# Gathering the tensor engine's small pieces of attention work in a two-layer hybrid trunk

## The chip, the cores and the metric

The kernel runs on one core of a Trainium2 chip. The metric is the device time of one execution in microseconds (us), from its first to its last instruction and what lies around them.

## The reference

Two layers, each a mixer sub-layer and a gated feed-forward, on x of 512 positions by 1024 channels, all in float32:

```python
for l in range(2):
    h = rms_norm(x, pre_mix_g[l])
    z = h @ w_in[l]                       # 1024 -> [u 512 | v 512 | q 512 | k 512 | values 512]
    u, v = gelu(z[u and v]); v = layer_norm(v)
    y_a = u * (W_s @ v + b)               # 4 groups, 128-position blocks, W_s block-lower-triangular
    # differential attention, 4 heads, two score maps a head (64 channels each), rotary on q and k,
    # 128-row blocks i = 0..3, chunk-causal mask of 64:
    p0, p1 = softmax(mask(q0 k0^T)), softmax(mask(q1 k1^T))
    y_b = rms_norm((p0 - lam * p1) @ values) * (1 - lam_init)
    x = x + rms_norm(concat(y_a, y_b) @ w_out[l])
    h = rms_norm(x)
    x = x + rms_norm((silu(h @ w_gate) * (h @ w_up)) @ w_down)
```

## The kernel before, in words

**Products.** A float32 product is made of three passes in fp32r: each operand is split in a high part and a low rest (`xg_hi`, `xg_lo`, `w_hi`, `w_lo`), and `product` (lines 604 to 606) issues high by high, high by low, low by high. These are the kernel's large matmuls, 512 columns wide in the mixer; this text calls them F. ScalarE makes `w_hi` from the raw weights (`high`, line 1078), GpSimd the rest (`low`, line 535), and SyncE's queue brings the weights, a chunk ahead.

**Small pieces.** The rest of TensorE's work in the mixer is small and lies between stretches of F. A score step n = 4 h + i (head h, row block i, 128 (i + 1) keys wide) goes through this chain:

- `scores(n)` on TensorE (line 669, "S" with its number): three fp32r passes for both maps into two PSUM banks.
- `maxima(n)` on VectorE (lines 1604, 1606): masks and takes the row maxima. `exponentials(n)` on ScalarE (line 1237). `combine(n)` on VectorE (lines 1613 to 1620): p0 - lam p1 into `attn`; its semaphore is `a_ready`.
- `turn(n)` on TensorE (line 682, "T"): i + 1 transposes of 128x128 in fp32. `copy_turned(n)` on ScalarE (lines 1246, 1249); its semaphore is `at_copied`. Steps i = 0 and i = 1 are copied together.
- `weigh(m)` on TensorE (line 697, "W"): steps 2m and 2m + 1 times the values, in fp32 (6 instructions for even m, 14 for odd m). `take_heads(m)` on ScalarE (lines 1258, 1259) takes the result out of the bank and sums its squares.

Each group g of the spatial gating has `gate(g)` (line 707, "G", 8 instructions), `add_terms(g)` on VectorE (line 1638, semaphore `gm_added`), and on u `copy_u(g)` and `u_gelus(g)` on ScalarE (lines 1269, 1273), `gated(g)` on GpSimd (line 542), `gated_high(g)` on ScalarE (line 1279) and `gated_low(g)` on GpSimd (line 546, semaphore `ya_ready`). Each head ends in `head_roots` (line 1264), `scale_head` on VectorE (line 1649, semaphore `o_scaled`), `turn_head(h)` on TensorE (line 714, "H"), `head_high` and `head_low` (lines 1283, 1654, semaphore `yb_ready`).

**The F stretches of the mixer**, in the order of the code: the gate's v, q and k tiles (`qk_half(n, lower or upper)`, 12 F each), the values (`va`), u (`u_half(t, ...)`, 12 F each), and the first half of the output product, `out_k(k)` for k = 0..7, 12 F each; `out_k(k)` waits for `ya_ready` k + 1 (k < 4) or for `yb_ready`. A tile of q or k is rotated after its product: `swapped(n)` on ScalarE (line 1219) waits for the tile's last F, `rotate(n)` on VectorE (lines 1585 to 1591), `rotated_high(n)` (line 1226), `rotated_low(n)` (line 1597, semaphore `qk_ready`).

**Order.** Each engine works through a list written out by hand, in order, once a layer; between them stand only semaphores. Nothing is scheduled at run time: a wait at the head of an engine's list holds all behind it. Before, step n's scores lie in banks 2 and 3 (even n) or 4 and 5 (odd n); bank 6 takes the turned tiles, bank 7 the weighed heads, and `scores(n)` waits for `a_ready` n - 1 (counted in the layer), that is for `combine(n - 2)`.

Of the kernel before, what the change touches and what calls it, by code (L numbers as in the profile page):

```python
# [15 lines left out]
P = 128  # L16
# [4 lines left out]
def trunk(nc, x, pre_mix_g, w_in, gmlp_ln_g, gmlp_ln_b, gmlp_ws, gmlp_b, lambda_q1, lambda_k1, lambda_q2,  # L21
# [41 lines left out]
    SC_BANKS = [(2, 3), (4, 5)]  # L63
    T_BANK, O_BANK = 6, 7

    GATE_BANKS = [2, 3, 4, 5]
# [8 lines left out]
    with ctx:  # L75
# [524 lines left out]
        def _(pe):  # L600
# [50 lines left out]
            def scores(l, n):  # L651
# [4 lines left out]
                if n == 0:  # L656
                    pe.wait_ge(vg_gelu, ST * l + 4)
                elif n == 8 or n == 9:

                    pe.wait_ge(gm_added, G * l + 2 * (n - 7))  # L660
                elif n > 1:

                    pe.wait_ge(a_ready, NS * l + n - 1)

                w = max(w, 2 * P)
                for n_pass, (q, k) in enumerate(((q_rot, k_rot), (q_low, k_rot), (q_rot, k_low))):
                    for j in range(2):
                        ps = slice(j * HD, (j + 1) * HD)
                        last = mm(bank[SC_BANKS[n % 2][j]][:, 0:w], q[ps, h, i * P:(i + 1) * P], k[ps, h, 0:w],  # L669
                                  start=(n_pass == 0), stop=(n_pass == 2))  # L670
                last.then_inc(sc_ready, 1)

            def turn(l, n):
                pe.wait_ge(a_ready, NS * l + n + 1)
                if n == 0:
                    pe.wait_ge(qk_ready, 8 * l + 3)
                elif n % ST != 1:
                    pe.wait_ge(at_copied, NS * l + n)

                at = 1 if n % ST == 1 else 0  # L680
                for k in range(n % ST + 1):
                    last = tr(b_tr[T_BANK][:, at + k, :], attn[n % 2][:, k * P:(k + 1) * P], ident[:, :])  # L682
                last.then_inc(at_ready, 1)

            def weigh(l, m):
# [6 lines left out]
                else:  # L692
                    pe.wait_ge(o_taken, 8 * l + m)
                for n in (2 * m, 2 * m + 1):
                    h, i = divmod(n, ST)
                    for k in range(i + 1):
                        last = mm(bank[O_BANK][:, (n % 2) * P:(n % 2 + 1) * P], attn_t(n, k),  # L697
# [3 lines left out]
            def gate(l, g):  # L701
# [3 lines left out]
                pe.wait_ge(a_ready, NS * l + (7 if g < 2 else 8))  # L705
# [176 lines left out]
            for l in range(L):  # L882
# [68 lines left out]
                turn(l, 2)  # L951
                va(C_VA + 1, 1, (0, 1))
                turn(l, 3)
# [17 lines left out]
                turn(l, 6)  # L971
                weigh(l, 1)
                qk_half(l, 4, upper)
                turn(l, 7)
                weigh(l, 2)
                qk_half(l, 5, lower)
                qk_half(l, 5, upper)
                for g in range(G):
                    gate(l, g)
                weigh(l, 3)  # L980
                qk_half(l, 6, lower)
                qk_half(l, 6, upper)
                scores_of_two(8)
# [6 lines left out]
                turn(l, 10)  # L990
                weigh(l, 4)
                u_half(l, 1, lower)
                turn(l, 11)
# [8 lines left out]
                turn(l, 14)  # L1002
                weigh(l, 6)
                u_half(l, 3, upper)
                turn(l, 15)
                out_k(l, 0)
                out_k(l, 1)
                weigh(l, 7)
                out_k(l, 2)
                turn_head(l, 0)  # L1010
                out_k(l, 3)
                turn_head(l, 1)
                turn_head(l, 2)
# [47 lines left out]
        def _(act):  # L1061
# [130 lines left out]
            for l in range(L):  # L1192
# [36 lines left out]
                def exponentials(n):  # L1229
                    w = (n % ST + 1) * P  # L1230
                    act.wait_ge(max_ready, NS * l + n + 1)
                    if n >= 2:
                        act.wait_ge(a_ready, NS * l + n - 1)
                    for j in range(2):
                        o = bank[SC_BANKS[n % 2][j]][:, 0:w]

# [3 lines left out]
                def copy_turned(n):  # L1240
# [4 lines left out]
                    if n % ST == 1:  # L1245
                        fn(attnT[:, 0:3 * P], bank[T_BANK][:, 0:3 * P], ACT.Copy).then_inc(at_copied, 2)
                    else:
                        w = (n % ST + 1) * P
                        fn(attnT[:, AT_AT[n % ST]:AT_AT[n % ST] + w], bank[T_BANK][:, 0:w], ACT.Copy)\
                            .then_inc(at_copied, 1)  # L1250

                def take_heads(m):

                    act.wait_ge(pv_ready, 8 * l + m + 1)
                    for n in (2 * m, 2 * m + 1):
                        h, i = divmod(n, ST)
                        o = bank[O_BANK][:, (n % 2) * P:(n % 2 + 1) * P]
                        fn(o_rows[:, i, h * P:(h + 1) * P], o, ACT.Copy, scale=rinv[:, n, 0:1])
                        last = fn(junk[:, (n % 2) * P:(n % 2 + 1) * P], o, ACT.Square, scale=rinv[:, n, 0:1], accum_out=o_ssq[:, h, i:i + 1])
# [55 lines left out]
                copy_turned(2)  # L1315
                copy_values(0)
                copy_values(1)
# [614 lines left out]
```

## Time and profile before

| | |
|---|---|
| median of 3 runs | 1087.63 us (1087.49 to 1087.68) |
| span of the profiled execution | 1085.3 us |
| instructions | 17599 |
| TensorE matmuls, busy | 1077.2 us, 99% of the span |
| VectorE / ScalarE / GpSimd busy | 601.7 / 585.8 / 573.9 us |
| chain that ended last | TensorE 99% |
| mean granted TensorE clock | 0.999 |

The profiled execution's span is counted from its first to its last instruction; the device time of the runs is 2.3 us above it. A matmul's duration in the rows overlaps with the next one's: what it costs is the distance from its start to the next one's start, and busy time on TensorE hides short pauses for the same reason.

### The profile page before, as it was taken

How to read it: one execution, taken by the hardware profiler on the slowest of the kernel's cores; microseconds unless marked ns; L12 is line 12 of the kernel's file. 1: busy time of each engine (PE TensorE's matmuls, PEld its weight loads, DVE VectorE, ACT ScalarE, POOL GpSimd, SP SyncE). 2: the span in 40 equal slices, each digit the busy share in tenths (PEclk: the TensorE clock that was granted, in tenths of full speed). 3: DMA queues.
4: the chain of work that ended last, by engine and by line, in shares of the span. 5: the costliest groups of instructions: out<-in, count | busy, mean ns of one | idle time of the engine just before them, and what ended most of it. 6: DMA issues, size and time to landing. Idle time of an engine off the chain costs nothing.

```text
span 1085.3 us, 17599 instructions
## 1 busy us (share of the span) xinstructions
PE 1077.2 (99%) x6840; PEld 968.0 (89%) x6840; DVE 601.7 (55%) x1011; ACT 585.8 (54%) x1143; POOL 573.9 (53%) x450
## 2 busy tenths in 40 slices
PE   8999999999999999999999999999999999999997
PEld 7878888999999999888888888889999999988886
DVE  4374544888888884010345646458888888820103
ACT  6767784666555554221457578656565555531212
POOL 3533264567666665544444234645766666655440
PEclk9999999999999999999999999999999999999999
DMA  8423212424433434522243222242443343263212
GB/s 281 137 65 92 78 56 82 155 79 117 117 97 100 117 100 169 178 97 97 86 143 102 78 79 78 68 125 81 118 117 97 98 117 103 93 215 121 96 55 77
DMA packets 144791, 118.33 MB, mean 109 GB/s; under 512 B 3754, under 2 KB 120004, under 8 KB 144708
## 3 DMA queue, kind: packets, MB, share of 16 engines
q1 hardware_dynamic: 144692, 117.20, 34.3%
q8 instruction: 54, 0.88, 0.3%
q14 instruction: 29, 0.24, 0.1%
q10 hardware_dynamic: 16, 0.00, 0.0%
HBM read 110.90 MB, written 6.29 MB: 108 GB/s over the span
## 4 chain that ended last, share of the span: by engine, by line
PE 99%; ACT 0%; DMA 0%; DVE 0%; issue 0%; DVEq 0%; ACTq 0%
PE banks L604 30%; PE banks L606 30%; PE banks L605 30%; PE banks L669 2%; PE banks L697 2%; PE banks L613 1%; PE banks L682 1%; PE banks L873 1%; PE banks L707 1%; DMA x_rows<-in_x_dram 0%; PE banks L714 0%; ACT junk L1086 0%; PE banks L964 0%; PE banks L958 0%; DVE scratch L1502 0%
## 5 line engine op out<-in xcount | busy, mean ns | idle before, releaser
L535 POOL TENSOR_TENSOR w_lo<-raw,w_hi 128x512 fp32r<-128x512 f32 x204 | 259.6, 1296 | 299.1 <-ACT w_hi L1078 299.1
L553 POOL TENSOR_TENSOR w_lo<-raw,w_hi 128x512 fp32r<-128x512 f32 x200 | 260.8, 1315 | 141.4 <-ACT w_hi L1147 137.0
L604 PE MATMUL banks<-xg_hi,w_hi 128*128 128x256 f32 (+1 forms) x896 | 276.3, 308 | 0.0
L606 PE MATMUL banks<-xg_lo,w_hi 128*128 128x256 f32 (+1 forms) x896 | 274.2, 306 | 0.0
L605 PE MATMUL banks<-xg_hi,w_lo 128*128 128x256 f32 (+1 forms) x896 | 274.0, 306 | 0.0
L1078 ACT ACTIVATE w_hi<-raw 128x1024 fp32r<-128x1024 f32 x102 | 107.0, 1060 | 161.4 <-PE banks L606 146.9
L1147 ACT ACTIVATE w_hi<-raw 128x512 fp32r<-128x512 f32 x200 | 125.1, 630 | 114.8 <-DVE raw L1795 61.1
L606 PEld LDWEIGHTS banks<-xg_lo,w_hi 128*128 128x128 f32 x896 | 171.2, 191 | 7.8
L604 PEld LDWEIGHTS banks<-xg_hi,w_hi 128*128 128x128 f32 x896 | 171.2, 191 | 7.7
L605 PEld LDWEIGHTS banks<-xg_hi,w_lo 128*128 128x128 f32 x896 | 171.3, 191 | 6.9
L604 PE MATMUL banks<-w_hi,hid_hi 128*128 128x512 f32 x352 | 137.2, 390 | 0.0
L606 PE MATMUL banks<-w_lo,hid_hi 128*128 128x512 f32 x352 | 137.0, 389 | 0.0
L605 PE MATMUL banks<-w_hi,hid_lo 128*128 128x512 f32 x352 | 137.0, 389 | 0.0
L604 PE MATMUL banks<-s_part,w_hi 128*128 128x256 f32 x480 | 135.8, 283 | 0.0
L605 PE MATMUL banks<-s_part,w_lo 128*128 128x256 f32 x480 | 135.8, 283 | 0.0
L606 PE MATMUL banks<-s_part,w_hi 128*128 128x256 f32 x480 | 135.8, 283 | 0.0
L604 PEld LDWEIGHTS banks<-s_part,w_hi 128*128 128x128 f32 x480 | 92.2, 192 | 0.0
L605 PEld LDWEIGHTS banks<-s_part,w_lo 128*128 128x128 f32 x480 | 92.2, 192 | 0.0
L606 PEld LDWEIGHTS banks<-s_part,w_hi 128*128 128x128 f32 x480 | 92.2, 192 | 0.0
L1801 DVE TENSOR_TENSOR w_lo<-banks,w_hi 128x512 fp32r<-128x512 f32 x80 | 54.9, 686 | 50.8 <-ACT w_hi L1147 50.8
L1524 DVE TENSOR_TENSOR banks<-banks,gpost 128x512 f32<-128x512 f32 x16 | 10.6, 696 | 126.6 <-ACT junk L1112 126.6
L606 PEld LDWEIGHTS banks<-w_lo,hid_hi 128*128 128x128 f32 x352 | 66.1, 188 | 13.9
(182 smaller groups left out, 1878.5 us busy)
## 6 DMA issues: line engine op xcount, KB each, us to landing
raw<-in_w_gate_up_dram SPq DMA_DIRECT2D x88, 512.0 KB, 4.1
raw<-in_w_down_dram SPq DMA_DIRECT2D x44, 512.0 KB, 3.5
raw<-in_w_in_dram SPq DMA_DIRECT2D x40, 512.0 KB, 3.8
raw<-in_w_out_dram SPq DMA_DIRECT2D x16, 512.0 KB, 3.5
x_spill<-x_rows SPq DMA_DIRECT2D x8, 512.0 KB, 4.3
x_rows<-x_spill SPq DMA_DIRECT2D x8, 512.0 KB, 4.7
x_rows<-in_x_dram SPq DMA_DIRECT2D x4, 512.0 KB, 7.4
out_dram<-x_rows SPq DMA_DIRECT2D x8, 256.0 KB, 2.0
```

The lines of the kernel that those rows point to most:

```text
L535: last = tt(lo[:, piece], raw_half(l, c, h)[:, piece], hi[:, piece].bitcast(F32), ALU.subtract)
L553: tt(lo, full, hi.bitcast(F32), ALU.subtract).then_inc(w_ready, 1)
L604: mm(o, stat[0], mov[0], start=first, stop=False)
L605: mm(o, stat[1], mov[0], start=False, stop=False)
L606: return mm(o, stat[0], mov[1], start=False, stop=last)
L613: last = tr(b_tr[turned_bank(group, r, half)][:, k, :], xn[:, r % 2, at:at + P], ident[:, :])
L669: last = mm(bank[SC_BANKS[n % 2][j]][:, 0:w], q[ps, h, i * P:(i + 1) * P], k[ps, h, 0:w], start=(n_pass == 0), stop=(n_pass == 2))
L682: last = tr(b_tr[T_BANK][:, at + k, :], attn[n % 2][:, k * P:(k + 1) * P], ident[:, :])
L697: last = mm(bank[O_BANK][:, (n % 2) * P:(n % 2 + 1) * P], attn_t(n, k), v_att[:, k, h * P:(h + 1) * P], start=(k == 0), stop=(k == i))
L1078: fn(high_low(l, c, h)[0], raw_half(l, c, h), ACT.Copy).then_inc(w_hi_ready, 1)
L1147: fn(factor(l, f, i)[0], full, ACT.Copy).then_inc(w_hi_ready, 1)
L1801: tt(lo, t_place(l, f, i), hi.bitcast(F32), ALU.subtract).then_inc(t_ready, 1)
```

## The change

The arithmetic stays the same. Three kinds of edit:

- **Banks.** Steps i = 0 and i = 1 of a head share banks 2 and 3 (columns 0 to 127 and 256 to 511), i = 2 uses them again, i = 3 has banks 4 and 5. So `maxima`, `exponentials` and `combine` of i = 0 now wait until step i = 1 has come as far too, and `scores` of i = 2 waits for `a_ready` n, that is for `combine(n - 1)`. Turned tiles of i = 3 go to bank 4, the others to bank 6. The weighed heads use all four quarters of bank 7, so that `weigh(1)` and `weigh(2)` can follow each other. `gate(3)` uses bank 5 after `gate(2)` and waits for `add_terms(2)`.
- **TensorE's order.** T2 and T3, T6 and T7, T10 and T11, T14 and T15 stand together; W1, W2 and three gates follow T7; W3, the last gate, S8 and S9 stand together behind the tile qk 6; T10, T11, W4, S12, S13 are one piece; T14, T15 and W6 come after u's last tile; W7 and H0 to H2 come after `out_k(2)`, and H3 after `out_k(4)`.
- **ScalarE's and VectorE's order** is changed to match: `copy_u(3)`, `copy_turned(14)`, `copy_turned(15)`, `take_heads(6)` now stand in this order before `u_gelus(2)`, `swapped(6)` before `take_heads(3)`, and on VectorE `rotate(6)` and `add_terms(3)` before `maxima(8)`.

The diff, with unchanged lines left out:

```diff
--- before.py
+++ after.py
@@ -60,10 +60,11 @@
...
-    SC_BANKS = [(2, 3), (4, 5)]
-    T_BANK, O_BANK = 6, 7
-
-    GATE_BANKS = [2, 3, 4, 5]
+    SC_AT = [(2, 0), (2, 256), (2, 0), (4, 0)]
+    T_BANKS_OF = [6, 6, 6, 4]
+    O_BANK = 7
+
+    GATE_BANKS = [2, 3, 5, 5]
@@ -655,31 +656,41 @@
...
                     pe.wait_ge(vg_gelu, ST * l + 4)
-                elif n == 8 or n == 9:
-
-                    pe.wait_ge(gm_added, G * l + 2 * (n - 7))
-                elif n > 1:
-
+                elif i == 0:
                     pe.wait_ge(a_ready, NS * l + n - 1)
+                elif i == 2:
+                    pe.wait_ge(a_ready, NS * l + n)
+                elif i == 3 and h > 0:
+
+                    pe.wait_ge(a_ready, NS * l + n - 3)
+                    pe.wait_ge(at_copied, NS * l + n - 3)
+                if h == 2 and i == 0:
+                    pe.wait_ge(gm_added, G * l + 2)
+                elif h == 2 and i == 3:
+                    pe.wait_ge(gm_added, G * l + 4)
                 w = max(w, 2 * P)
+                b, at = SC_AT[i]
                 for n_pass, (q, k) in enumerate(((q_rot, k_rot), (q_low, k_rot), (q_rot, k_low))):
...
                         ps = slice(j * HD, (j + 1) * HD)
-                        last = mm(bank[SC_BANKS[n % 2][j]][:, 0:w], q[ps, h, i * P:(i + 1) * P], k[ps, h, 0:w],
+                        last = mm(bank[b + j][:, at:at + w], q[ps, h, i * P:(i + 1) * P], k[ps, h, 0:w],
                                   start=(n_pass == 0), stop=(n_pass == 2))
...
                 pe.wait_ge(a_ready, NS * l + n + 1)
+                i = n % ST
                 if n == 0:
                     pe.wait_ge(qk_ready, 8 * l + 3)
-                elif n % ST != 1:
+                elif i == 0:
+                    pe.wait_ge(at_copied, NS * l + n - 1)
+                elif i == 2:
                     pe.wait_ge(at_copied, NS * l + n)
-                at = 1 if n % ST == 1 else 0
-                for k in range(n % ST + 1):
-                    last = tr(b_tr[T_BANK][:, at + k, :], attn[n % 2][:, k * P:(k + 1) * P], ident[:, :])
+                at = 1 if i == 1 else 0
+                for k in range(i + 1):
+                    last = tr(b_tr[T_BANKS_OF[i]][:, at + k, :], attn[n % 2][:, k * P:(k + 1) * P], ident[:, :])
                 last.then_inc(at_ready, 1)
@@ -689,12 +700,12 @@
...
                     pe.wait_ge(add_ready, l + 1)
-                else:
+                elif m != 2:
                     pe.wait_ge(o_taken, 8 * l + m)
...
                     for k in range(i + 1):
-                        last = mm(bank[O_BANK][:, (n % 2) * P:(n % 2 + 1) * P], attn_t(n, k),
+                        last = mm(b_tr[O_BANK][:, n % ST, :], attn_t(n, k),
                                   v_att[:, k, h * P:(h + 1) * P], start=(k == 0), stop=(k == i))
@@ -702,7 +713,10 @@
...
-                pe.wait_ge(a_ready, NS * l + (7 if g < 2 else 8))
+                if g < 3:
+                    pe.wait_ge(a_ready, NS * l + (7 if g < 2 else 8))
+                else:
+                    pe.wait_ge(gm_added, G * l + 3)
                 for n in range(ST):
@@ -948,9 +962,8 @@
...
                 va(C_VA + 1, 0, (0, 1))
-                turn(l, 2)
                 va(C_VA + 1, 1, (0, 1))
-                turn(l, 3)
+                turn_two(2)
@@ -968,18 +981,18 @@
...
                 qk_half(l, 4, lower)
-                turn(l, 6)
+                qk_half(l, 4, upper)
+                turn_two(6)
                 weigh(l, 1)
-                qk_half(l, 4, upper)
-                turn(l, 7)
                 weigh(l, 2)
+                for g in range(3):
+                    gate(l, g)
                 qk_half(l, 5, lower)
                 qk_half(l, 5, upper)
-                for g in range(G):
-                    gate(l, g)
-                weigh(l, 3)
                 qk_half(l, 6, lower)
                 qk_half(l, 6, upper)
+                weigh(l, 3)
+                gate(l, 3)
                 scores_of_two(8)
@@ -987,10 +1000,9 @@
...
                 u_half(l, 0, upper)
-                turn(l, 10)
+                u_half(l, 1, lower)
+                turn_two(10)
                 weigh(l, 4)
-                u_half(l, 1, lower)
-                turn(l, 11)
                 scores_of_two(12)
@@ -999,18 +1011,15 @@
...
                 u_half(l, 3, lower)
-                turn(l, 14)
+                u_half(l, 3, upper)
+                turn_two(14)
                 weigh(l, 6)
-                u_half(l, 3, upper)
-                turn(l, 15)
-                out_k(l, 0)
-                out_k(l, 1)
+                for k in range(3):
+                    out_k(l, k)
                 weigh(l, 7)
-                out_k(l, 2)
-                turn_head(l, 0)
+                for h in range(H - 1):
+                    turn_head(l, h)
                 out_k(l, 3)
-                turn_head(l, 1)
-                turn_head(l, 2)
                 out_k(l, 4)
@@ -1228,11 +1237,12 @@
...
                     w = (n % ST + 1) * P
-                    act.wait_ge(max_ready, NS * l + n + 1)
+                    act.wait_ge(max_ready, NS * l + n + (2 if n % ST == 0 else 1))
                     if n >= 2:
                         act.wait_ge(a_ready, NS * l + n - 1)
+                    b, at = SC_AT[n % ST]
                     for j in range(2):
-                        o = bank[SC_BANKS[n % 2][j]][:, 0:w]
+                        o = bank[b + j][:, at:at + w]
@@ -1243,20 +1253,20 @@
...
                     if n % ST == 1:
-                        fn(attnT[:, 0:3 * P], bank[T_BANK][:, 0:3 * P], ACT.Copy).then_inc(at_copied, 2)
+                        fn(attnT[:, 0:3 * P], bank[T_BANKS_OF[1]][:, 0:3 * P], ACT.Copy).then_inc(at_copied, 2)
                     else:
                         w = (n % ST + 1) * P
-                        fn(attnT[:, AT_AT[n % ST]:AT_AT[n % ST] + w], bank[T_BANK][:, 0:w], ACT.Copy)\
+                        fn(attnT[:, AT_AT[n % ST]:AT_AT[n % ST] + w], bank[T_BANKS_OF[n % ST]][:, 0:w], ACT.Copy)\
                             .then_inc(at_copied, 1)
...
-                    act.wait_ge(pv_ready, 8 * l + m + 1)
+                    act.wait_ge(pv_ready, 8 * l + m + (2 if m == 1 else 1))
                     for n in (2 * m, 2 * m + 1):
                         h, i = divmod(n, ST)
-                        o = bank[O_BANK][:, (n % 2) * P:(n % 2 + 1) * P]
+                        o = b_tr[O_BANK][:, n % ST, :]
                         fn(o_rows[:, i, h * P:(h + 1) * P], o, ACT.Copy, scale=rinv[:, n, 0:1])
-                        last = fn(junk[:, (n % 2) * P:(n % 2 + 1) * P], o, ACT.Square, scale=rinv[:, n, 0:1], accum_out=o_ssq[:, h, i:i + 1])
+                        last = fn(junk[:, (n % ST) * P:(n % ST + 1) * P], o, ACT.Square, scale=rinv[:, n, 0:1], accum_out=o_ssq[:, h, i:i + 1])
                     last.then_inc(o_taken, 1)
@@ -1312,9 +1322,9 @@
...
                 rotated_high(3)
-                copy_turned(2)
                 copy_values(0)
                 copy_values(1)
+                copy_turned(2)
                 copy_turned(3)
@@ -1330,21 +1340,21 @@
...
                 high(l, 7, 1)
+                swapped(4)
                 copy_turned(6)
+                copy_turned(7)
                 take_heads(1)
-                swapped(4)
-                copy_turned(7)
                 take_heads(2)
...
                 rotated_high(5)
+                swapped(6)
                 take_heads(3)
-                swapped(6)
+                rotated_high(6)
                 exponentials(8)
                 exponentials(9)
-                rotated_high(6)
                 high(l, 9, 0)
@@ -1353,10 +1363,10 @@
...
                 copy_u(0)
+                high(l, 10, 0)
                 copy_turned(10)
+                copy_turned(11)
                 take_heads(4)
-                high(l, 10, 0)
-                copy_turned(11)
                 exponentials(12)
@@ -1371,20 +1381,20 @@
...
                 gated_high(1)
+                copy_u(3)
                 copy_turned(14)
+                copy_turned(15)
                 take_heads(6)
-                copy_u(3)
-                copy_turned(15)
                 u_gelus(2)
...
                 high(l, 11, 1)
+                high(l, 12, 0)
                 take_heads(7)
...
                 head_high(0)
-                high(l, 12, 0)
                 head_high(1)
@@ -1598,18 +1608,20 @@
...
                 def maxima(n):
-                    b, w = SC_BANKS[n % 2][0], (n % ST + 1) * P
-                    dve.wait_ge(sc_ready, NS * l + n + 1)
-
-                    nc.vector.memset(banks[0:CH, b:b + 2, w - CH:w], NEG_INF).then_inc(sc_masked, 1)
+                    b, at = SC_AT[n % ST]
+                    to = at + (n % ST + 1) * P
+                    dve.wait_ge(sc_ready, NS * l + n + (2 if n % ST == 0 else 1))
+
+                    nc.vector.memset(banks[0:CH, b:b + 2, to - CH:to], NEG_INF).then_inc(sc_masked, 1)
                     dve.wait_ge(sc_masked, NS * l + n + 1)
-                    nc.vector.tensor_reduce(nmx[:, n, :], banks[:, b:b + 2, 0:w], AX_X, ALU.max, negate=True)\
+                    nc.vector.tensor_reduce(nmx[:, n, :], banks[:, b:b + 2, at:to], AX_X, ALU.max, negate=True)\
                         .then_inc(max_ready, 1)
...
+                    b, at = SC_AT[n % ST]
                     w = (n % ST + 1) * P
-                    dve.wait_ge(exp_done, 2 * (NS * l + n + 1))
+                    dve.wait_ge(exp_done, 2 * (NS * l + n + (2 if n % ST == 0 else 1)))
                     nc.vector.reciprocal(rinv[:, n, :], psumr[:, n, :]).then_inc(rinv_ready, 1)
@@ -1617,7 +1629,7 @@
...
                         dve.wait_ge(at_ready, NS * l + n - 1)
-                    stt(attn[n % 2][:, 0:w], bank[SC_BANKS[n % 2][1]][:, 0:w], cw[:, n:n + 1], prob[n % 2][:, 0:w],
+                    stt(attn[n % 2][:, 0:w], bank[b + 1][:, at:at + w], cw[:, n:n + 1], prob[n % 2][:, 0:w],
                         ALU.mult, ALU.add).then_inc(a_ready, 1)
@@ -1710,18 +1722,18 @@
...
                 rotated_low(4)
-                rotate(5)
                 add_terms(0)
                 add_terms(1)
+                add_terms(2)
+                rotate(5)
                 rotated_low(5)
-                add_terms(2)
+                rotate(6)
                 add_terms(3)
...
                 maxima(9)
-                rotate(6)
+                rotated_low(6)
                 combine(8)
                 combine(9)
-                rotated_low(6)
                 maxima(10)
```

## Rows read from the trace of the kernel before

**Rows 1.** The page, busy time of TensorE over the whole span.
```profile
PE 1077.2 (99%) x6840; PEld 968.0 (89%) x6840; DVE 601.7 (55%) x1011; ACT 585.8 (54%) x1143; POOL 573.9 (53%) x450
```

**Rows 2.** Waits on TensorE, whole span: us in total, times, longest us.
```profile
PE banks L613 <- DVE scratch L1498: 1.2, 1, 1.2
```

**Rows 3.** Timeline of TensorE, layer 0, u's last tiles and out: start, us.
```profile
145.30 0.49 PE L682 MATMUL banks<-ident,scratch 128*128 128x128 f32 x3
...
146.22 0.47 PE L604 MATMUL banks<-xg_hi,w_hi 128*128 128x512 f32 x1
...
149.07 0.60 PE L682 MATMUL banks<-ident,scratch 128*128 128x128 f32 x4
...
155.00 1.72 PE L697 MATMUL banks<-v_att,attnT 128*128 128x128 f32 x14
156.48 0.48 PE L604 MATMUL banks<-w_hi,ya_hi 128*128 128x512 f32 x1
...
162.53 1.03 PE L714 MATMUL banks<-ident,o_rows 128*128 128x128 f32 x8
```

**Rows 4.** Timeline of TensorE, layer 0: qk 6, S8, qk 7, S10; six F between its first rows.
```profile
110.06 0.39 PE L606 MATMUL banks<-xg_lo,w_hi 128*128 128x512 f32 x1
...
111.42 0.39 PE L606 MATMUL banks<-xg_lo,w_hi 128*128 128x512 f32 x1
111.73 0.38 PE L669 MATMUL banks<-k_rot,q_rot 64*128 64x256 f32 x2
...
112.64 0.50 PE L604 MATMUL banks<-xg_hi,w_hi 128*128 128x512 f32 x1
...
118.31 0.44 PE L669 MATMUL banks<-k_rot,q_rot 64*128 64x384 f32 x2
```

**Rows 5.** Timeline of VectorE, layer 0, gating terms, steps 8 and 9.
```profile
105.64 1.40 DVE L1638 SCALAR_TENSOR_TENSOR v_gate<-banks,par,add_t 128x512 f32<-128x512 f32 x2
...
112.46 0.17 DVE L1604 MEMSET banks<- 64x128 f32 x1 [3.50 <-PE banks L669]
...
113.30 0.69 DVE L1606 TENSOR_REDUCE nmx<-banks 128x2 f32<-128x512 f32 x1
114.26 0.70 DVE L1585 TENSOR_TENSOR banks<-banks,trig 128x512 f32<-128x512 f32 x1 [0.28 <-ACT swap L1219]
...
116.27 0.15 DVE L1613 RECIPROCAL rinv<-psumr 128x2 f32<-128x2 f32 x1
...
117.53 0.48 DVE L1620 SCALAR_TENSOR_TENSOR scratch<-banks,cw,scratch 128x256 f32<-128x256 f32 x1
```

**Rows 6.** Timeline of ScalarE, layer 0, tile qk 6, steps 8 and 9.
```profile
111.84 2.39 ACT L1219 ACTIVATE swap<-banks 32x512 f32<-32x512 f32 x4 [4.17 <-PE banks L606]
114.26 0.37 ACT L1237 ACTIVATE scratch<-banks,nmx 128x128 f32<-128x128 f32 x1
...
115.76 0.21 ACT L1237 ACTIVATION_READ_ACCUMULATOR banks<-banks,nmx 128x1 f32 x1
```

**Rows 7.** Timeline of ScalarE, layer 0, `take_heads(6)` and the table load for gelu.
```profile
146.50 0.37 ACT L1258 ACTIVATE o_rows<-banks,rinv 128x128 f32<-128x128 f32 x1 [0.18 <-PE banks L697]
...
147.61 0.21 ACT L1259 ACTIVATION_READ_ACCUMULATOR junk<-banks,rinv 128x1 f32 x1
...
150.37 1.28 ACT L1273 ACT_TABLE_LOAD   x1
```

**Rows 8.** Timeline of GpSimd, layer 0, `gated` and `gated_low` of groups 2 and 3.
```profile
152.44 2.54 POOL L542 TENSOR_TENSOR uT<-uT,v_gate 128x512 f32<-128x512 f32 x2 [2.54 <-ACT uT L1273]
155.04 2.60 POOL L546 TENSOR_TENSOR ya_lo<-uT,ya_hi 128x512 fp32r<-128x512 f32 x2
```

**Rows 9.** Timeline of VectorE, layer 0, heads 0 to 2 scaled.
```profile
154.73 6.66 DVE L1649 TENSOR_SCALAR o_rows<-o_rows,o_rs 128x128 f32<-128x128 f32 x12
```

**Rows 10.** Waits of TensorE's weight loads, whole span: us in total, times, longest us.
```profile
PEld banks L682 <- issue: 2.9, 8, 0.4
```

**Rows 11.** Window view, 6 to 8 us; after the busy times: granted clock, DMA, GB/s.
```profile
6.00:8.00 2.00, 1.27 (x11) 1.27 (x12) 1.04 (x3) 1.34 (x3) 1.08 (x1) 1.00 1.00 370
```

## The prediction

> **What bounds the kernel now.** I read the page first, then the waits, then the timelines of the mixer, since the change touches nothing else. TensorE is busy 99% of the span [rows 1], and its longest wait in the whole execution is 1.2 us, at the launch [rows 2]; in the mixer it waits for nobody. VectorE, ScalarE and GpSimd are busy little more than half the time, but the hand-written lists let TensorE meet them with small margins, and what counts here are these margins. So the time can move in two ways only: TensorE's own sequence gets shorter, or it starts to wait. Work saved on another engine is worth nothing by itself. Both layers run the same list, so each term counts twice.
>
> **What gathering saves.** An F costs 0.227 us: six lie between 110.06 and 111.42 [rows 4]. Behind a small piece the stretch of F is longer than that: 12 F from 146.22 to 149.07 take 2.85 us where 12 x 0.227 is 2.72 [rows 3]. So a return to F costs 0.13. Part of it is given back: T of three tiles with W6 takes 0.92 (145.30 to 146.22), while four more transposes behind four others add 1.03 - 0.60 = 0.43, that is 0.108 each, by which nine instructions would take 0.97 [rows 3]. The last small instruction before F is thus cheaper by 0.05, or by 0.07 if a weighing instruction costs 0.110, the value that I take below; so one piece fewer saves some 0.06. Counting the lists: before, a layer has 20 separate pieces between stretches of F; after, 13 (T2 joins T3; T6 W1, T7 W2, the gates with W3 and S8 S9 become two; T10 W4 joins T11 S12 S13; T14 W6 joins T15; W7, H0, H1 H2 become one). Seven fewer, in two layers 14: 14 x 0.06 = 0.8 us. Bounds: nothing, and 14 x 0.13 = 1.8 us. The small instructions themselves are all still there.
>
> **First new wait: S10.** `scores(10)` has i = 2. Before, it waited for `combine(8)`, and S11 for `combine(9)`; now S10 waits for `combine(9)`. In front of it, `swapped(6)`, `rotate(6)` and `add_terms(3)` now stand before `maxima(8)` and the exponentials of steps 8 and 9. Before, `maxima(8)` went ahead as soon as S8 was there (112.46) while ScalarE was still swapping tile 6 (111.84 to 114.23) [rows 5, 6]; these two ran side by side, and now they follow one another. I count from E, the end of the F of qk 6 (111.73 in rows 4).
>
> - VectorE and ScalarE: swap starts at E + 0.2 (0.11 in the rows, where the step from F to S holds some 0.1), 2.42 to the next ScalarE instruction (111.84 to 114.26) [rows 6]; rotate 2.01 (114.26 to 116.27); `add_terms(3)` 0.66 to 0.70 (two take 1.40); `maxima` of 8 and 9 is 113.30 + 0.69 - 112.46 = 1.53 [rows 5]; 0.04 to ScalarE; the exponentials of both, which `combine(8)` now awaits together, 115.76 + 0.21 - 114.26 = 1.71 [rows 6]; 0.04 back; both combines 117.53 + 0.48 - 116.27 = 1.74 [rows 5]. With 0.07 until TensorE starts (an estimate) the sum is E + 10.4.
> - TensorE: W3 and G3, 22 instructions at 0.11, 2.4 us (14 of W7 take 1.48 [rows 3]); 0.1 for the step to S; S8 and S9 0.91 (111.73 to 112.64); qk 7 5.67 (112.64 to 118.31) [rows 4]. It is at S10 at E + 9.1.
>
> TensorE waits 1.3 us, and behind S10 everything on it is held: S11, T8, T9, u. By the same count the earlier order had `combine(9)` at 118.01 [rows 5] against S10 at 118.31 [rows 4], so there was no wait. Bounds: 1.0 and 1.7, since no row shows this sequence as a whole. The later chains start from TensorE's own outputs and move with it, so nothing of this is won back: TensorE has no idle time left to give.
>
> **Second new wait: `out_k(2)`.** It needs `gated_low(2)` on GpSimd, which hangs on `u_gelus(2)` on ScalarE. Now `copy_turned(14)` and `take_heads(6)` stand between `copy_u(3)` and the gelu, and `take_heads(6)` waits for W6, which itself now comes only after u's last tile, T14 and T15. I count from U, the end of u's last F (149.07, where T15 began before [rows 3]).
>
> - ScalarE and GpSimd before: table load for gelu at 150.37 = U + 1.30 [rows 7], `gated_low(2)` from 155.04, half of 2.60 for one of the two: ready at 156.34 = U + 7.27 [rows 8]. TensorE came to `out_k(2)` at 156.48 = U + 7.41 [rows 3], 0.14 later.
> - After: T14 T15 W6 take 0.92 + 0.43 = 1.35 [rows 3]; `take_heads(6)` starts 0.28 behind W6's end (146.50 against 146.22) and holds ScalarE 1.2 (146.50 to about 147.7) [rows 3, 7]. The table load starts at U + 2.8 instead of 1.3, 1.5 us later, and `gated` with both `gated_low` and `gated_high` shifts with it: ready at U + 8.8, seen at 8.86.
> - TensorE after: 1.35, then 24 F with one return, 24 x 0.227 + 0.13 = 5.58, make U + 6.93. W7 no longer stands ahead of `out_k(2)` as filler.
>
> TensorE waits 1.9 us. Bounds: 1.6 and 2.3. Queued behind it are W7 and the heads. H2 needs head 2 scaled: before at 154.73 + 6.66 = 161.39 = U + 12.3 [rows 9], now 1.5 later, U + 13.8; TensorE reaches H2 at 8.86 + 2.85 + 1.56 + 0.86 = U + 14.1. Taken as no wait, 0.3 as its upper bound.
>
> **The other edits, costed at nothing.** The shared banks delay the exponentials of steps 0, 4 and 12 by the maxima of the next step, and the combines with them. For step 12 the sum of the same prices is: S12's start + 0.91 + 0.3 to VectorE, 1.53 + 1.71 + 1.74 and the hand-overs give about + 6.1, against S14 at 0.91 + 5.67 = + 6.6 by [rows 4]. If that cover were gone it would cost up to 0.3. S2 and S6 have their combines by the same count, S2 with hardly any spare; up to 0.1. u's second tile loses the piece T10 W4 ahead of it, 0.92 + 0.13, and comes that much closer behind `rotated_low(7)`; up to 0.2. T6, T7, W1, W2 and the gates move later than their inputs, and G3's wait for `add_terms(2)` is met while qk 6 runs. No DMA is moved on SyncE's queue, and GpSimd's list is unchanged.
>
> **Sum.** 2 x (1.3 + 1.9) - 0.8 = +5.6 us. The profiled execution of before has a span of 1085.3 and runs took 2.3 us more; so a span of 1090.9 and a time of 1087.63 + 5.6 = 1093.2 us. Its own range: 2 x 2.6 - 1.8 = +3.4 to 2 x (1.7 + 2.3 + 0.3) = +8.6, that is 1091.0 to 1096.2.
>
> **Rivals.** A measurement of this kernel tells 0.2% (2.2 us) from no change.
>
> - *Only one wait is real* (9%). The two chains are separate. If GpSimd and ScalarE are late as computed but VectorE makes S10 in time: 2 x 1.9 - 0.8, 1090.6. If only S10 waits: 2 x 1.3 - 0.8, 1089.4, within 0.2%. For it: I added single prices. Against it: the spare before was 0.14 and 0.3, and each chain grows by over a microsecond.
> - *Not slower: the pieces cost much more than I take* (5%). The weight loads pause 0.36 us at a transpose piece (2.9 us in 8 cases [rows 10]). If that is what a piece costs, gathering gives 14 x 0.36 = 5.0, and the time is 1087.6 + 6.4 - 5.0 = 1089.0. It decides from 0.30 per piece (inside 0.2%), break-even at 0.46. Against it: the starts of the matmuls, not of the loads, set the time, and these show 0.13 at most.
> - *Faster or the same: the waits don't bind* (4%). If VectorE and ScalarE are released earlier than their lists say, only the saving stays: 1086.8, at best 1085.8.
> - *The clock falls in the pauses* (4%). After a wait of 1.2 us [rows 2] the granted clock stood at 1.00, the level of 2.4 GHz, in the window from 6 to 8 us [rows 11]. The new waits are longer, 1.9. If TensorE fell to 1.2 GHz after each of the four for as long as ten F, each would cost 10 x 0.227 = 2.3 more: 1102.4. The Trainium skill (TensorE: Matmul & The Clock Gate, "HAM oscillation — how this bites in real kernels") says that pauses between bursts of matmuls can put the engine back to the half clock; so far as this trace goes it stays up.
>
> **How the numbers follow.** Forecast 78%, the rivals 9, 5, 4 and 4%. The range of 8 in 10 is 1089.9 to 1096.4: it takes in the forecast's bounds and the case with the second wait alone. Slower by over 0.2%: 78 + 6 (of the first rival) + 4 = 88%. Within 0.2%: 9%. Faster: 3%.
>
> **What would show it.** In the profile after: TensorE with waits in the mixer, in each layer one before S10 (line of the scores, released by VectorE's last combine instruction) of some 1.3 us, and one before the F of `out_k(2)`, released by GpSimd's `gated_low`, of 1.9. 12 F behind a piece still take 2.85, and a layer has 13 pieces. The table load for the second gelu starts 2.8 us after u's last F. Wrong would be: TensorE without idle time in the mixer; a wait at H2, W7 or u's second tile of over half a microsecond; the stretches of F shorter by more than 0.13 for each piece gone; a mean clock visibly below 1.

## The result: 1097.82 us, and the profile after

The changed kernel takes **1097.82 us** (4 runs, 1097.72 to 1097.97), the kernel before 1087.6 us beside it: a ratio of 1.0094 (95% interval 1.0082 to 1.0106). It is slower, as forecast, but by 10.2 us and not by 5.6; the time lies above the range given.

The page of the profiled execution after; its span is 1095.7 us, 10.4 above that of before. It answers to [rows 1]:

```profile
PE 1081.6 (99%) x6840; PEld 971.8 (89%) x6840; DVE 601.9 (55%) x1011; ACT 583.6 (53%) x1143; POOL 574.4 (52%) x450
```

This line tells little: the share of TensorE is the same, and its busy time is 4.4 us longer although it does the same 6840 matmuls. The waits on TensorE (us in total, times, longest), against [rows 2]:

```profile
PE banks L605 <- POOL ya_lo L547: 3.9, 2, 2.0
PE banks L677 <- DVE scratch L1632: 2.6, 2, 1.3
PE banks L857 <- DVE eps L1493: 1.2, 1, 1.2
```

The third is at the launch and is 1.2 us in the kernel before too; the launch wait that [rows 2] shows is 0.5 here. The first two are the two waits forecast, at `out_k(2)` and at S10. Together they are 6.5 us, and gathering takes something off; so some 4 us of the slowdown are in no row of this view. To find them I measured the stretches from the start of one matmul to the start of another, the same ones in both traces. From the first score step to the first F behind H3, before takes 112.91 us in layer 0 and 112.75 in layer 1, after 117.93 and 117.91; every other stretch agrees within 0.1 us. So all of it is in the attention part, 5.0 to 5.2 us a layer. Now TensorE after, layer 0, behind the second wait (start, us, and in brackets the idle time and its releaser), against the rows from 156.48 on in [rows 3]:

```profile
117.78 0.39 PE L607 MATMUL banks<-xg_lo,w_hi 128*128 128x512 f32 x1
119.49 0.45 PE L677 MATMUL banks<-k_rot,q_rot 64*128 64x384 f32 x2 [1.32 <-DVE scratch L1632]
...
155.86 0.39 PE L607 MATMUL banks<-w_lo,ya_hi 128*128 128x512 f32 x1
158.22 0.50 PE L605 MATMUL banks<-w_hi,ya_hi 128*128 128x512 f32 x1 [1.97 <-POOL ya_lo L547]
...
159.86 0.63 PE L605 MATMUL banks<-w_hi,ya_hi 128*128 128x512 f32 x1
160.29 0.63 PE L606 MATMUL banks<-w_hi,ya_lo 128*128 128x512 f32 x1
...
162.42 1.98 PE L708 MATMUL banks<-v_att,attnT 128*128 128x128 f32 x14
164.23 1.69 PE L728 MATMUL banks<-ident,o_rows 128*128 128x128 f32 x12
165.68 0.47 PE L605 MATMUL banks<-w_hi,ya_hi 128*128 128x512 f32 x1
```

By start to start, S10 comes 1.71 us behind the last F; two starts here would be 0.32 apart without a wait, so it costs 1.39. `out_k(2)` comes at 2.36 instead of 0.23: 2.13. From 158.22 to the F behind H2 it is 7.46 us; in the variant with the gelu first, below, in which TensorE runs the same list there, it is 161.77 - 156.09 = 5.68, so 1.78 are lost in this piece. Layer 1 has 7.47 and 5.68. The sum 1.39 + 2.13 + 1.78 = 5.30 against the measured 5.02 leaves 0.28 for gathering.

Two things happen in that piece. First, from 159.86 on the F start 0.43 apart instead of 0.23. The windows of after there (bounds in us, sum, busy time and count of PE, PEld, DVE, ACT, POOL, then the granted clock, the share and rate of the DMA):

```profile
158.00:159.00 1.00, 0.78 (x3) 0.67 (x4) 1.00 (x2) 1.00 (x2) 1.00 (x2) 1.00 0.00 0
...
161.00:162.00 1.00, 1.00 (x4) 0.71 (x4) 1.00 (x2) 0.00 (x0) 1.00 (x2) 0.50 0.00 0
...
163.00:164.00 1.00, 1.00 (x11) 1.00 (x10) 1.00 (x2) 0.00 (x0) 1.00 (x2) 1.00 0.65 238
```

The granted clock is 0.50, the level of 1.2 GHz, from some 1.3 us after TensorE resumed until about 162.9; in layer 1 it falls again, there within 0.2 us of the resumption (698.69) and until about 702.2. Second, the scaling of heads 0 to 2 on VectorE, 6.66 us in [rows 9], takes 8.69 here, beside GpSimd, which works without a break:

```profile
156.52 8.69 DVE L1661 TENSOR_SCALAR o_rows<-o_rows,o_rs 128x128 f32<-128x128 f32 x12
```

```profile
154.22 2.54 POOL L543 TENSOR_TENSOR uT<-uT,v_gate 128x512 f32<-128x512 f32 x2 [2.90 <-ACT uT L1283]
156.82 2.60 POOL L547 TENSOR_TENSOR ya_lo<-uT,ya_hi 128x512 fp32r<-128x512 f32 x2
159.38 4.96 POOL L536 TENSOR_TENSOR w_lo<-raw,w_hi 128x512 fp32r<-128x512 f32 x4
```

The heads are scaled at 156.52 + 8.69 = 165.21, and the F behind H2 starts 0.47 later. Either event could be the one that costs; which one, the experiments had to say.

### The profile page after: what moved, and what is told of

It reads as the page before. It is cut to its first block, busy times and chain, and to the rows that moved or that the text cites. A ratio compares the mean times of both kernels' runs of the same rounds, so it can differ in the third digit from the quotient of the medians.

```text
span 1095.7 us, 17595 instructions
## 1 busy us (share of the span) xinstructions
PE 1081.6 (99%) x6840; PEld 971.8 (89%) x6840; DVE 601.9 (55%) x1011; ACT 583.6 (53%) x1143; POOL 574.4 (52%) x450
## 4 chain that ended last, share of the span: by engine, by line
PE 95%; ACT 2%; DVE 1%; POOL 1%; issue 0%; DMA 0%; DVEq 0%; ACTq 0%; POOLq 0%
PE banks L605 30%; PE banks L607 29%; PE banks L606 29%; PE banks L677 2%; PE banks L614 1%; PE banks L708 1%; PE banks L887 1%; PE banks L693 1%; PE banks L721 0%; ACT swap L1228 0%; PE banks L728 0%; DMA x_rows<-in_x_dram 0%; POOL uT L543 0%; POOL ya_lo L547 0%; ACT L1283 0%
## 5 line engine op out<-in xcount | busy, mean ns | idle before, releaser
L605 PEld LDWEIGHTS banks<-w_hi,hid_hi 128*128 128x128 f32 x352 | 66.1, 188 | 13.8 <-POOL w_lo L536 0.3
```

Of the source, the lines that this page charges most:

```text
L605: mm(o, stat[0], mov[0], start=first, stop=False)
```

## The experiments

All times are medians beside runs of the kernel before on the same chip (1087.6 to 1087.7 us).

**1. Gelu first.** ScalarE's list puts both gelus and what follows them back ahead of step 14; all else as after.

```diff
                 copy_u(3)
-                copy_turned(14)
-                copy_turned(15)
-                take_heads(6)
                 u_gelus(2)
                 ...
                 gated_high(3)
+                copy_turned(14)
+                copy_turned(15)
+                take_heads(6)
```

> The changed kernel with ScalarE's list alone edited: both gelus of u, the head roots and gated_high(2), gated_high(3) stand straight behind copy_u(3), ahead of copy_turned(14), copy_turned(15) and take_heads(6). Theory A (ScalarE's list makes the wait at out_k(2), and that wait brings the half clock): the wait of 2.0 us goes in both layers and the stretch at 1.2 GHz with it; 1097.8 minus 2 x 2.1 minus 2 x 1.6 gives 1090.4, TensorE's clock 1.00 all through. Rival B (the half clock comes from the gathered fp32 pieces ahead of it, not from the wait): only the wait goes, 1093.6, and the clock still reads 0.50 near there. Rival C (GpSimd is the bound, not ScalarE's order): no change, 1097.8.

**1089.98 us**, ratio 1.0021 (1.0012 to 1.0031). The wait at `out_k(2)` is gone, that at S10 is left at 1.3 us each time. So this one order of ScalarE holds 7.8 of the 10.2 us, twice as much as the wait that is listed for it. `high(12,0)` has its new place here too, yet the heads are scaled in 6.66 us:

```profile
154.33 6.66 DVE L1661 TENSOR_SCALAR o_rows<-o_rows,o_rs 128x128 f32<-128x128 f32 x12
```

since GpSimd gets a break of 1.09 us ahead of `low(11,1)`, while ScalarE does `take_heads(6)`. The time lies within half a microsecond of theory A's 1090.4, but that is luck: the theory took 1.6 us a layer for the half clock, and experiment 4 shows that this was not what it cost.

**2. Steps first.** VectorE's and ScalarE's lists take steps 8 and 9 ahead of the end of tile 6.

```diff
-                rotate(6)
-                add_terms(3)
                 maxima(8)
                 maxima(9)
-                rotated_low(6)
+                rotate(6)
+                add_terms(3)
                 combine(8)
                 combine(9)
+                rotated_low(6)
```

(and `rotated_high(6)` behind `exponentials(9)` on ScalarE)

> The changed kernel with VectorE's and ScalarE's lists edited around steps 8 and 9 alone: maxima(8), maxima(9) ahead of rotate(6), add_terms(3); exponentials(8), (9) ahead of rotated_high(6); combine(8), (9) ahead of rotated_low(6). The shared banks stay. Theory A (the list order makes the wait at S10): the wait of 1.3 us goes in both layers, 1097.8 minus 2.8 gives 1095.0, the rest as it was. Rival D (the shared banks, by which S10 needs combine(9) and exponentials(8) need maxima(9), make it): at least 0.5 us of wait stays in each layer, 1096.5 or more.

**1095.84 us**, 1.0076 (1.0059 to 1.0093). The wait at S10 falls from 1.3 to 0.3 and takes its 2 us along; theory A had it gone whole (1095.0), rival D had over 0.5 left. In this profile the clock stayed at 1.00 behind `out_k(2)`, with the same wait of 2.0 us, and something else appears on TensorE:

```profile
PE banks L605 <- POOL ya_lo L547: 3.9, 2, 2.0
PE banks L728 <- DVE o_rows L1661: 2.5, 2, 1.2
```

The second row is H1 waiting for its scaled head. The four runs had mean clocks of 0.999, 0.997, 0.995 and 0.999 and took 1095.89, 1095.78, 1096.15 and 1095.79 us: they differ in the clock and hardly in the time.

**3. Both.** The two edits together.

> Both edits of lists together, TensorE's gathered order and the banks as in the changed kernel. Theory A: all new waits and the half clock gone, what is left is what gathering gives: 1087.6 minus 0.4 to 0.8, 1086.8 to 1087.2. Rival E (gathering has a cost of its own that the waits hid, such as heads 0 to 2 late for their turning): 1087.6 or more, up to 1089.

**1088.03 us**, 1.0003 (0.9994 to 1.0013): no change from before. A wait of 0.3 us at S10 is left in each layer, which the expectation had not counted.

**4. A filler.** After, with 8 unused F between `out_k(1)` and `out_k(2)`, so that TensorE works on while it waits.

```diff
-                for k in range(3):
+                for k in range(2):
                     out_k(l, k)
+                for _ in range(8):
+                    mm(bank[5][:, :], ya_hi[:, 0, 0:P], ya_hi[:, 0, :], start=True, stop=True)
+                out_k(l, 2)
```

> The changed kernel with eight matmuls of 512 columns more on TensorE, between out_k(1) and out_k(2), into a bank that is free there; their result is not used. They take 8 x 0.227 = 1.8 us of the 2.0 us wait. If the wait itself brings the half clock: TensorE's wait is down to 0.3 us, the clock stays at 1.00, and with more work the kernel is faster by 2 x 1.6: 1094.6. If the half clock comes from elsewhere: 1097.8, clock 0.50 as before.

**1097.94 us**, 1.0095 (1.008 to 1.011): not a microsecond back. The expectation that the half clock was the cost failed. The filler did what it should: the wait at `out_k(2)` is 0.2, the clock stays at 1.00 (0.999 to 1.0 in four runs). But TensorE then waits at H1:

```profile
162.70 0.60 PE L728 MATMUL banks<-ident,o_rows 128*128 128x128 f32 x4
164.55 1.44 PE L728 MATMUL banks<-ident,o_rows 128*128 128x128 f32 x8 [1.25 <-DVE o_rows L1664]
165.75 0.48 PE L605 MATMUL banks<-w_hi,ya_hi 128*128 128x512 f32 x1
```

The F behind H2 starts at 165.75, in after at 165.68. With the clock halved or not, TensorE gets past H2 when VectorE has scaled the heads (here 156.55 + 8.73 = 165.28). In after the matmuls at half clock fill this time, and so no view lists a wait.

**5. `high(12,0)` later**, back behind `head_high(0)`, all else as after, so that GpSimd's next piece of work comes later.

```diff
                 high(l, 11, 1)
-                high(l, 12, 0)
                 take_heads(7)
                 ...
                 head_high(0)
+                high(l, 12, 0)
```

> The changed kernel with one instruction of ScalarE's list moved: high(12, 0) stands behind head_high(0) again, as before the change, instead of ahead of take_heads(7). Nothing else. In the changed kernel GpSimd worked without a pause from 154.2 to 164.3 us, and VectorE's twelve instructions that scale heads 0 to 2 took 8.7 us, where before they took 6.7; one of them takes 0.27 us alone and up to 1.33 beside GpSimd. Theory F (VectorE is held by GpSimd's low(12, 0), and late heads set the end of this stage, whatever the clock does): the twelve take 6.7 or less, TensorE's wait for the heads goes, and the time is 1087.6 plus 2 x (1.4 + 2.1) minus 0.6, 1094.0, where the clock stays at 1.00; each layer in which it falls to 0.50 costs 1.6, so up to 1097.2. Rival G (the late heads come from the later table load alone): the twelve still take over 8 us, 1097.8.

**1096.18 us**, 1.0079 (1.0064 to 1.0094). Heads 0 to 2 are scaled in 6.64 us again and H1 waits no more, but the same meeting comes back one head later: VectorE scales head 3 beside `low(12,0)`, in 4.01 us where [rows 9]' kernel took 2.52, and H3 waits 0.5.

```profile
156.56 6.64 DVE L1661 TENSOR_SCALAR o_rows<-o_rows,o_rs 128x128 f32<-128x128 f32 x12
...
166.03 4.01 DVE L1661 TENSOR_SCALAR o_rows<-o_rows,o_rs 128x128 f32<-128x128 f32 x4
```

The waits at S10 and `out_k(2)` are those of after (1.3 and 2.0); its four runs show clocks of 0.999 to 1.0. The expectation was 1094.0, 2.2 us less: it had no place for H3. From the last F before H3 to the first behind it is 1.53 us here and 0.58 in experiment 4, so H3 costs 0.95 us a layer, 1.9 of the 2.2.

**6. Both 4 and 5.**

> e5 and the eight filler matmuls of e4 together, so that the wait at out_k(2) is 0.2 instead of 2.0 us. Theory F with the wait as the cause of the half clock: the clock reads 1.00 in both layers, no wait for the heads, 1094.0. If e5 is above it, the difference is the price of the half clock, 1.6 for each layer. Rival G: 1097.8 with a wait of 1.2 us for the heads in each layer, as in e4.

**1096.22 us**, 1.0078 (1.0062 to 1.0095): the same as without the filler, which again only fills the wait.

**7. `high(12,0)` early, in the kernel before**, alone:

```diff
                 high(l, 11, 1)
+                high(l, 12, 0)
                 take_heads(7)
                 ...
                 head_high(0)
-                high(l, 12, 0)
```

> The kernel before with high(12, 0) moved ahead of take_heads(7), the only edit. Theory F: GpSimd's low(12, 0) runs on behind low(11, 1) from 160.1 to 162.7 us, the last five scaling instructions take until about 163.9 instead of 161.4, and TensorE, which comes to H2 at 163.0, waits 0.9 us in each layer: 1087.6 plus 1.8 gives 1089.4. Rival G: no change, 1087.6.

**1089.55 us**, 1.0018 (1.0008 to 1.0027). The heads are slow here too, with nothing else changed:

```profile
154.78 8.78 DVE L1649 TENSOR_SCALAR o_rows<-o_rows,o_rs 128x128 f32<-128x128 f32 x12
```

The move of one line on ScalarE costs 0.9 us a layer by itself (the stretch from the first score step to the F behind H3 takes 113.85 against 112.91), although the gelu is on time here and 12 more F stand ahead of H1 and H2 than in after.

**8. Shared score banks, in the kernel before**, alone (banks, columns and waits of the scores, maxima, exponentials and combines; the lists as before).

> The kernel before with the shared score banks alone: steps 0 and 1 of a head in banks 2 and 3, step 2 there again, step 3 in banks 4 and 5, and the waits that go with them; every list keeps its order and every other bank stays. Theory A (the order of the lists makes the wait at S10): combine(9) still ends at 118.0 and S10 comes at 118.3, so at most 0.1 us of wait, 1087.6 to 1088.0. Rival D (the banks make it): over half a microsecond of wait at S10 in each layer, 1088.8 or more. In e2, with the banks and the lists turned back, 0.3 us was left in each layer, so something between is possible.

**1087.51 us**, 0.9999 (0.999 to 1.0008). The banks cost nothing while the lists around them stay.

**9. Experiment 3 with `add_terms(3)` ahead of `maxima(8)`.**

> e3 with one VectorE instruction moved: add_terms(3) stands ahead of maxima(8), where VectorE sat idle for 3 us in e3, instead of between rotate(6) and combine(8). In e3 TensorE still waited 0.35 us at S10 in each layer. Theory A: that wait goes, 1088.03 minus 0.7 gives 1087.3, and what is left against the kernel before is what gathering 14 pieces is worth, 0.3 to 0.7 us, within what can be told from no change. Rival D (the wait comes from the shared banks): 1088.0 as in e3.

**1087.15 us** (11 runs, 1086.93 to 1087.29), 0.9995 (0.9986 to 1.0004). No wait is left in the mixer. What stands is what gathering is worth: 0.5 us in the medians. All 11 runs lie below all 21 of the kernel before beside them (1087.55 to 1087.92), yet the interval includes no change. The stretch of the attention part takes 112.56 in both layers against 112.91 and 112.75, so 0.35 and 0.19. It is the fastest of all kernels run, and no measurable gain.

**10 and 11. The wait by itself, in the kernel before**, with nothing gathered: two, and four, unused copies of 512 columns on ScalarE ahead of `u_gelus(2)`, each waited for, make `out_k(2)` late.

```diff
+                for n in range(4):
+                    fn(junk[:, HALF:D], x_rows[:, 0, 0:HALF], ACT.Copy).then_inc(held_back, 1)
+                    act.wait_ge(held_back, 4 * l + n + 1)
                 u_gelus(2)
```

> The kernel before with two copies of 512 columns put on ScalarE ahead of u_gelus(2), their result unused, which make the chain to out_k(2) 1.2 us later. The chain had 0.14 us to spare, so TensorE waits 1.05 us in each layer: 1087.6 plus 2.1 gives 1089.7. If a wait of this length brings the half clock, up to 1.6 more for each layer, 1092.9; if the heads are held more than out_k(2), more than 2.1 as well.

> The same with four copies, 2.4 us: TensorE waits 2.2 us in each layer, 1087.6 plus 4.4 gives 1092.0 where the clock stays at 1.00. Here the heads have room behind the wait, so a stretch at 1.2 GHz is not hidden: each costs 1.6 and shows as 0.0015 in the mean clock of that run, up to 1095.2. If the runs with a lower mean clock are not longer, the half clock costs nothing here either.

Two copies: **1090.02 us**, 1.0022 (1.0013 to 1.0031), waits of 0.9 us, clock 0.999 to 1.0 in ten runs. Four: 1094.27 us, 1.0066 (1.0053 to 1.0078), waits of 2.2 us. Its five runs lie in two groups, 1094.20, 1094.26 and 1094.27 us (clock 0.997 to 0.998), and 1095.50 and 1095.72 (0.996). In its profile, TensorE resumes after the same wait in both layers, at 159.28 and at 697.04:

```profile
159.28 0.51 PE L605 MATMUL banks<-w_hi,ya_hi 128*128 128x512 f32 x1 [2.18 <-POOL ya_lo L547]
159.62 0.40 PE L606 MATMUL banks<-w_hi,ya_lo 128*128 128x512 f32 x1
...
697.04 0.79 PE L605 MATMUL banks<-w_hi,ya_hi 128*128 128x512 f32 x1 [2.18 <-POOL ya_lo L547]
697.63 0.63 PE L606 MATMUL banks<-w_hi,ya_lo 128*128 128x512 f32 x1
```

In layer 0 the clock stays at 1.00 and the 12 F and H0 take 3.25 us (to 162.53); in layer 1 it is at 0.50 for over three microseconds, and they take 4.70 (to 701.74). So a fall costs up to 1.45 us where nothing hides it, and the distance between the two groups of runs, 1.2 to 1.5 us, would fit a second fall (no profile of the slower group is there to show it); the attention part as a whole is 1.29 longer in layer 1 (116.67 against 115.38).

## Why the prediction was right, and where it failed

- **S10: right.** 1.3 forecast, 1.39 measured. In after `combine(9)` ends at 118.95 + 0.48 = 119.43 and S10 starts at 119.49, 10.5 behind the end of qk 6 (108.98, where W3 starts), against E + 10.4 in the sum. Experiment 2 shows that the order on VectorE and ScalarE makes it, experiment 8 that the shared banks alone do not. The last row of `combine(9)` in after:

```profile
118.95 0.48 DVE L1632 SCALAR_TENSOR_TENSOR scratch<-banks,cw,scratch 128x256 f32<-128x256 f32 x1
```

- **`out_k(2)`: right, a little small.** The table load for the gelu was forecast at U + 2.8; u's last F ends at 149.18 (U) and the load starts at 152.16, U + 2.98. The wait costs 2.13 against 1.9, within the bounds.

```profile
152.16 1.28 ACT L1283 ACT_TABLE_LOAD   x1
```

- **Gathering: right.** 0.4 us a layer forecast; 0.28 by the account above, 0.19 to 0.35 in experiment 9.
- **The score banks and the gates: right**, no cost (experiment 8 and the waits of experiment 9).
- **The heads: this step failed.** I wrote "H2 needs head 2 scaled: before at 154.73 + 6.66 = 161.39 = U + 12.3 [rows 9], now 1.5 later, U + 13.8 ... Taken as no wait", and "GpSimd's list is unchanged". GpSimd's list is, but not its times: `high(12,0)` moved ahead of `take_heads(7)` on ScalarE, an edit that I gave no price, and it is what `low(12,0)` on GpSimd hangs on. GpSimd then runs through, and VectorE with it takes 8.69 instead of 6.66. The heads are there at 165.21 = U + 16.0; TensorE without a wait would be at H2 at U + 14.1 by the forecast, at U + 14.3 by the distances in experiment 1. So the term that was put at nothing is 1.7 to 1.9 us a layer, measured 1.78. Of the missing 4.6 us this makes 3.6, the small excess of the two waits 0.6, the smaller gain of gathering 0.2, and layer 1, whose attention part grows by 5.16 and not by 5.02, another 0.1.

The sign that was to show it, a wait at H2 of over half a microsecond, is in no list of the profile; the other one is, a mean clock below 1 (0.996 to 0.998).

What makes VectorE slow can be read from the durations of its scaling instructions (ns: least, median, most) in before and in after:

```profile
L1649 DVE TENSOR_SCALAR o_rows<-o_rows,o_rs x16: 274/278/1328, 154.7 to 164.4; 128x128 f32<-128x128 f32 x16
```

```profile
L1661 DVE TENSOR_SCALAR o_rows<-o_rows,o_rs x16: 274/283/1326, 156.5 to 168.2; 128x128 f32<-128x128 f32 x16
```

Alone, one takes 0.27 us; beside GpSimd up to 1.33, about the length of one of GpSimd's (1.30). Read one by one, of the twelve of heads 0 to 2 four take about 1.3 us before, and six after; each of these starts 0.04 to 0.15 us behind the start of an instruction of GpSimd and ends within 0.1 us behind its end. 6.66 us was not the price of twelve scalings (12 x 0.27 = 3.3) but the price beside four instructions of GpSimd; after, it is beside six. This agrees with the Trainium skill ("SBUF — State Buffer", section "Who interferes with whom"): a `tensor_scalar` and a GpSimd instruction can need the same pair of ports, whoever starts first has it for the whole instruction, and the other is blocked. I had not brought that rule to this place.

- **The rival "the clock falls in the pauses"** (4%, 1102.4). It fell, twice in the profiled execution, after the two waits of 2.0 us and not after those of 1.3 at S10. It cost nothing there, since the time it takes lies under VectorE's lateness: experiment 4 removes the fall and wins nothing, and the runs of experiment 2 take the same time at different clocks. Had the heads been on time, it would have cost some 1.3 to 1.45 us each (an estimate from experiment 11, another kernel).
- **The others** did not come about: both waits are real, the pieces cost less than thought, nothing was faster.

**The two causes overlap**, and this is why they can't be added up. Experiment 1 removes the wait at `out_k(2)` and the late heads together and gives 7.8 us. It does the second not by the gelu alone: experiment 7 has the gelu on time and slow heads all the same. It also puts `take_heads(6)` between `gated_high(3)` and `high(11,1)`, which gives GpSimd its break. Experiment 5 removes the contention for heads 0 to 2 alone and gives 1.6 and not 3.6, because H3 takes back 0.95 a layer.

**Open.** What decides whether the clock falls after a wait of 2.0 to 2.2 us. Experiment 5 has the waits of after and four runs at 0.999 or above; experiment 11 has both cases in one execution. The kernels with no wait beyond 1.3 us in the mixer (experiments 1, 3, 7 to 10) show no mean clock below 0.998 in any run, and the kernel before has 0.998 too.

## What to carry to other kernels

The duration of an instruction taken from a row holds beside the work that ran next to it there. Before such a row is used for another order, divide it by its count and look at the least and the most. Here they differ by five times, and the price depended on the neighbour; then one must ask when the neighbour will run now. An engine whose list is unchanged still moves if what releases it moves: follow each moved instruction to those that wait for it. And a cost seen in a trace (here the half clock) is only paid if nothing later is waited for anyway: fill the pause and see whether the time comes back.

## What was not expected of the hardware

- The granted clock fell to 0.50 some 1.3 us after TensorE had resumed from a wait of 2.0 us (after) and, in another kernel, during the wait of 2.2 (experiment 11, layer 1); in both it stayed there for about three microseconds. Equal waits in the same execution did and did not bring it about.
- Where a fall hits, TensorE's busy time grows by what the F take longer: this, not more work, is part of the 4.4 us that the page shows after.
- A VectorE instruction of 0.27 us was held up to 1.33 us by a neighbour on GpSimd, instruction by instruction for eight microseconds.
